# Second near inverse in two pieces, row sums on GpSimd, third o block loaded whole: the recurrence of a two-block network

## The reference, cut to what matters

```python
def step(state, xs):           # over the tokens
    sa = einsum('bhvk,bhk->bhv', state, a_t)
    state = (state * w_t[:, :, None, :] + sa[..., None] * b_t[:, :, None, :]
             + v_t[..., None] * k_t[:, :, None, :])
    return state, einsum('bhvk,bhk->bhv', state, r_t)
...
y = groupnorm_per_head(y) * ln_w + ln_b
y = y + sum(r * k * r_k, per head) * v          # bonus
return (y * g) @ w_o, v_first
```

## Time and profile before

| | |
|---|---|
| median of 3 runs | 1130.73 us |
| profiled execution, its own time | 1129.51 us |
| span of the profiled execution | 1127.5 us |
| TensorE, VectorE, ScalarE, GpSimd busy | 97%, 72%, 49%, 4% of the span |
| mean granted clock of TensorE | 0.995 of full speed |

### The profile page before, as it was taken

How to read it: one execution, slowest core, us unless ns; L and a number is a source line. 1 busy time by engine, 2 the same in 40 slices (tenths; PEclk the granted TensorE clock), 3 DMA queues, 4 the chain that set the end, 5 groups by cost and what they waited for, 6 DMA issues and landing times.

```text
span 1127.5 us, 18637 instructions
## 1 busy us (share of the span) xinstructions
PE 1096.3 (97%) x7454; PEld 914.5 (81%) x7454; DVE 816.5 (72%) x1161; ACT 553.5 (49%) x690; POOL 43.3 (4%) x50
## 2 busy tenths in 40 slices
PE   9999999999999887899999999999999999999998
PEld 7887888889778667787888888798977888989896
DVE  4664544538579795979999987999997977555554
ACT  6545633436455425364334356465554756444443
POOL 0000000000000420101111100000000000000000
PEclk9999999999999989999999999999999999999999
DMA  9585456453344221649989963374540654564633
GB/s 337 192 267 187 152 183 223 157 179 112 113 149 136 74 42 41 260 153 374 341 321 343 347 212 115 111 226 149 167 149 2 202 161 133 177 207 166 208 127 112
DMA packets 138141, 205.86 MB, mean 183 GB/s; under 512 B 19592, under 2 KB 95645, under 8 KB 138078
## 3 DMA queue, kind: packets, MB, share of 16 engines
q1 hardware_dynamic: 130644, 177.63, 47.9%
q0 software_dynamic: 6560, 25.19, 5.9%
q10 hardware_dynamic: 874, 2.15, 0.5%
HBM read 202.33 MB, written 1.57 MB: 181 GB/s over the span
## 4 chain that ended last, share of the span: by engine, by line
PE 86%; DVE 8%; ACT 2%; DMA 2%; issue 1%; ACTq 0%; DVEq 0%
PE ps L749 24%; PE ps L751 24%; PE ps L750 24%; PE ps L975 2%; DVE wl L2532 1%; PE ps L1193 1%; PE ps L1632 1%; DMA raw<-in_ab_w_in 1%; PE ps L826 1%; PE ps L1108 1%; PE ps L1460 1%; PE ps L1107 1%; PE ps L1132 1%; PE ps L1614 1%; DVE wide L2646 1%
## 5 line engine op out<-in xcount | busy, mean ns | idle before, releaser
L2532 DVE TENSOR_TENSOR wl<-raw,wh 128x2048 fp32r<-128x2048 f32 (+2 forms) x154 | 345.4, 2248 | 98.5 <-ACT wh L1755 98.1
L749 PE MATMUL ps<-wh,xh 128*128 128x512 f32 (+3 forms) x856 | 339.0, 396 | 2.7 <-DVE wl L2532 1.4
L751 PE MATMUL ps<-wl,xh 128*128 128x512 f32 (+3 forms) x856 | 332.2, 388 | 0.0
L750 PE MATMUL ps<-wh,xl 128*128 128x512 f32 (+3 forms) x856 | 332.0, 388 | 0.0
L1755 ACT ACTIVATE wh<-raw 128x2048 fp32r<-128x2048 f32 (+2 forms) x154 | 286.7, 1878 | 41.0 <-PE ps L751 31.0
L749 PEld LDWEIGHTS ps<-wh,xh 128*128 128x128 f32 x856 | 161.4, 189 | 39.3 <-issue 2.4
L751 PEld LDWEIGHTS ps<-wl,xh 128*128 128x128 f32 x856 | 161.3, 188 | 34.8
L750 PEld LDWEIGHTS ps<-wh,xl 128*128 128x128 f32 x856 | 161.5, 189 | 33.3 <-issue 1.0
L749 PE MATMUL ps<-wh,gh 128*128 128x512 f32 x288 | 114.1, 396 | 0.8 <-DVE wl L2532 0.8
L751 PE MATMUL ps<-wl,gh 128*128 128x512 f32 x288 | 113.8, 395 | 0.0
L750 PE MATMUL ps<-wh,gl 128*128 128x512 f32 x288 | 113.6, 395 | 0.0
(11 more groups left out here) (448 smaller groups left out, 1307.1 us busy)
## 6 DMA issues: line engine op xcount, KB each, us to landing
wide<-in_w_ada POOLq DMA_DIRECT2D x24, 1024.0 KB, 9.2
raw<-in_ffn_w_gate SPq DMA_DIRECT2D x44, 512.0 KB, 4.4
raw<-in_ffn_w_up SPq DMA_DIRECT2D x44, 512.0 KB, 5.5
raw<-in_ffn_w_down SPq DMA_DIRECT2D x22, 1024.0 KB, 5.0
raw<-in_w_mlp_in SPq DMA_DIRECT2D x16, 1024.0 KB, 7.3
raw<-in_w_mlp_out SPq DMA_DIRECT2D x16, 1024.0 KB, 5.1
raw<-in_w_in SPq DMA_DIRECT2D x16, 512.0 KB, 4.8
raw<-in_w_in SPq DMA_DIRECT2D x8, 1024.0 KB, 5.0
```

What stands on the lines that cost most here:

```text
L749: pe.matmul(o, lh, rh, start=start, stop=False)
L750: pe.matmul(o, ll, rh, start=False, stop=False)
L751: return pe.matmul(o, lh, rl, start=False, stop=stop)
L2532: v.tensor_tensor(wl[:, s, 0:width], raw[:, s, 0:width], f32(wh[:, s, 0:width]), ALU.subtract).then_inc(lo_ready[s], 1)
```

## The change

1. `near_blocks` keeps only its two multiplications. The sums are made by GpSimd in `near_rows(g)`: an addition of 256 elements in each partition, then one of 128. `near_in` waits for these. GpSimd runs `near_rows(0)`, `(1)` after the first four fold steps, and `(2)`, `(3)` after the other four.
2. VectorE takes `mask_b` of a group right behind its `near_blocks`.
3. GpSimd's gate steps no longer wait for `near(0)`; those of the second half wait for both `y1_out(0)` and `(1)`.
4. `near` stops after the left product for corners of 8. The right product (`near_last`) follows at once for the first inverse, and for the second only after `r4_out(1)`. The halves of the first and the second o block are split later on VectorE.
5. SyncE issues `a_columns((2, 3))` ahead of `near_out(1)`, and the third o block as one load of 1 MB; ScalarE splits it between `gkv_out(2)` and `gkv_out(3)` instead of after `r1_out(3)`.
6. The four near buffers are allocated last in SBUF, so what lay behind them moves down by 3456 bytes in each partition.

```diff
@@ make_plan
-    for (n, k), s, dmas in zip(O_ORDER, (2, 0, 1, 2), (1, 1, 4, 1)):
+    for (n, k), s, dmas in zip(O_ORDER, (2, 0, 1, 2), (1, 1, 1, 1)):
@@ SyncE, recurrence_loads
                 near_in(1)
+                a_columns((2, 3))
                 near_out(1)
-                a_columns((2, 3))
                 sp.wait_ge(S("gate_T"), B("gate_T") + 4)
-                in_pieces(("o",) + O_ORDER[2], 2)
+                in_place(("o",) + O_ORDER[2])
@@ SyncE, near_in
-                sp.wait_ge(S("wkv.nc"), B("wkv.nc") + 2 * hh + 2)
+                sp.wait_ge(S("near_rows"), B("near_rows") + 4 * hh + 4)
@@ GpSimd
+            def near_rows(g):
+                blocks = tmps[g]["xt"].rearrange("p (y u b c) -> p y u b c", y=2, u=4, b=4)
+                pairs = tmps[g]["xt"].rearrange("p (u n) -> p u n", u=8)
+                rows = NEAR_ROWS(W, g // 2).rearrange("p (y g u c) -> p y g u c", y=2, g=2, u=4)[:, :, g % 2]
+                pool.wait_ge(S("wkv.nc"), B("wkv.nc") + g + 1)
+                nc.gpsimd.tensor_tensor(pairs[:, :, 0:32], pairs[:, :, 0:32], pairs[:, :, 32:64], ALU.add).then_inc(S("near_rows"), 1)
+                pool.wait_ge(S("near_rows"), B("near_rows") + 2 * g + 1)
+                nc.gpsimd.tensor_tensor(rows, blocks[:, :, :, 0, :], blocks[:, :, :, 1, :], ALU.add).then_inc(S("near_rows"), 1)
...
+                if hh == 0:
+                    near_rows(0)
+                    near_rows(1)
+            near_rows(2)
+            near_rows(3)
...
-            pool.wait_ge(S("wkv.near"), B("wkv.near") + 1)
             for hh in range(2):
...
                 pool.wait_ge(S("gate_out"), B("gate_out") + 2 * (hh + 1))
+                if hh:
+                    pool.wait_ge(S("wkv.y1"), B("wkv.y1") + 2)
@@ ScalarE
             for g in (0, 2):
                 if g == 2:
                     gkv_out(2)
+                    act.wait_ge(S("fold"), B("fold") + 16)
+                    split_in_place(("o",) + O_ORDER[2])
                     gkv_out(3)
...
                 r1_out(g + 1)
-                if g == 2:
-                    act.wait_ge(S("fold"), B("fold") + 16)
-                    split_in_place(("o",) + O_ORDER[2])
@@ VectorE, near_blocks
-                link(m)
-                rows = NEAR_ROWS(W, g // 2).rearrange("p (y g u c) -> p y g u c", y=2, g=2, u=4)
-                for y in range(2):
-                    m = v.tensor_reduce(rows[:, y, g % 2], ..., AX_X, ALU.add)
@@ VectorE, near
+                left_product(4)
+                right_product(4)
+                left_product(8)
+
+            def near_last():
+                right_product(8, last=True)
@@ VectorE, inverse_out
+                else:
+                    v.wait_ge(S("near_rows"), B("near_rows") + 2 * g + 6)
@@ VectorE, the order
             for g in (0, 2):
-                for step in (near_blocks, mask_b, mask_k, mask_x):
+                for i in (g, g + 1):
+                    near_blocks(i)
+                    mask_b(i)
+                for step in (mask_k, mask_x):
                     step(g)
                     step(g + 1)
                 if g == 0:
                     near(0)
+                    near_last()
...
                 y1_out(g)
-                if g == 0:
-                    split_in_place(first, 0)
-                else:
+                if g == 2:
                     centre(0, 0)
                 y1_out(g + 1)
...
                 r4_out(g)
-                if g == 0:
-                    split_in_place(first, 1)
-                    split_in_place(second, 0)
-                else:
+                if g == 2:
                     centre(0, 1)
                     variance(0, 0)
                     variance(0, 1)
                 r4_out(g + 1)
                 if g == 0:
-                    split_in_place(second, 1)
+                    near_last()
+                    split_in_place(first, 0)
                 else:
                     gated(0, 0)
                 q_out(g)
-                if g == 2:
+                if g == 0:
+                    split_in_place(first, 1)
+                else:
                     gated(0, 1)
                 q_out(g + 1)
...
                 state_out(g)
                 state_out(g + 1)
+                if g == 0:
+                    split_in_place(second, 0)
+                    split_in_place(second, 1)
```

More of the change, by code:

```diff
@@ L123 @@
     "pool_1": (("ones", 1), ("fold", 16)),
-    "pool_2": (("lowr_one", 1), ("near_zero", 1), ("near_unit", 1)),
+    "pool_2": (("lowr_one", 1), ("near_zero", 1), ("near_unit", 1), ("near_rows", 8)),
     "pe_1": (("cols_T", 1), ("y_T", 4)),
@@ L359, in build @@
         posi = sb("posi", [P, NT], I32)
+        near_m = sb("near_m", [P, NEAR])
+        near_u = sb("near_u", [P, NEAR])
+        near_c = sb("near_c", [P, 2 * P])
+        near_p = sb("near_p", [P, 64])
         ps = ctx.enter_context(nc.psum_tensor("ps", [P, 8, 512], F32))
@@ L504, in in_place @@
                   .then_inc(raw_loaded[s], 16)
-            def in_pieces(name, g, pieces=range(4)):
-                s, use, _, _ = plan.at[name]
-                sp.wait_ge(w_used[s], use)
-                for a in pieces:
-                    step = ("wkv.gkv", "wkv.mt", "wkv.r1", "wkv.m2")[a]
-                    sp.wait_ge(S(step), B(step) + g + 1)
-                    r0, n0 = name[2] * 512 + a * P, name[1] * 512
-                    sp.dma_start(wl_plain[:, s * SLOT + a * 512:s * SLOT + (a + 1) * 512], SRC["o"][r0:r0 + P, n0:n0 + 512])\
-                      .then_inc(raw_loaded[s], 16)
             def recurrence_loads():
@@ L2990, in mask_k, with corners, near_part, small_products @@
                                 mask_two("strict_st", "upto_st"), ALU.mult).then_inc(S("wkv.gk"), 1)
+            def corners(s):
+                k = 8 // s
+                u, m = [t[:, :].rearrange("p (k z) -> p k z", k=k)[:, :, 0:32 * s].rearrange("p k (i c) -> p k i c", c=16) for t in (near_u, near_m)]
+                return u[:, :, 0:s, 0:s], u[:, :, 0:s, s:2 * s], u[:, :, s:2 * s, s:2 * s], m[:, :, 0:s, s:2 * s]
+            def near_part(s):
+                return near_p[:, 0:8 * s].rearrange("p (k i c) -> p k i c", i=s, c=s)
+            def small_products(s, a, b, o):
+                k = 8 // s
+                products = W(8, 0, k * s ** 3).rearrange("p (k i c j) -> p k i c j", k=k, i=s, c=s)
+                for n in range(k):
+                    m = v.tensor_tensor(products[:, n], a[:, n].unsqueeze(2).to_broadcast([P, s, s, s]),
+                                        b[:, n].rearrange("p j c -> p c j").unsqueeze(1).to_broadcast([P, s, s, s]), ALU.mult)
+                link(m)
+                for n in range(k):
+                    m = v.tensor_reduce(o[:, n], products[:, n], AX_X, ALU.add)
+                return m
+            def left_product(s):
+                _, _, u22, m12 = corners(s)
+                link(small_products(s, m12, u22, near_part(s)))
+            def right_product(s, last=False):
+                u11, u12, _, _ = corners(s)
+                m = small_products(s, u11, near_part(s), u12)
+                if last:
+                    m.then_inc(S("wkv.near"), 1)
+                else:
+                    link(m)
             def near(hh):
@@ L2998, in near @@
                     v.wait_ge(S("near_unit"), B("near_unit") + 1)
-                def corners(s):
-                    k = 8 // s
-                    u, m = [t[:, :].rearrange("p (k z) -> p k z", k=k)[:, :, 0:32 * s].rearrange("p k (i c) -> p k i c", c=16) for t in (near_u, near_m)]
-                    return u[:, :, 0:s, 0:s], u[:, :, 0:s, s:2 * s], u[:, :, s:2 * s, s:2 * s], m[:, :, 0:s, s:2 * s]
                 _, u12, _, m12 = corners(1)
```

22 lines of the change are left out of this document (2 added, 20 removed).

## The result

The changed kernel takes 1110.3 us (median of 4 runs, 1109.84 to 1110.7) against 1130.54 us (4 runs, 1129.19 to 1132.53): ratio 0.982, 95% interval 0.980 to 0.983. The profiled execution took 1110.59 us, with a span of 1108.4 us.

The account below looks back on a forecast made before the run. TensorE, busy 97% of the span, was taken to bound the kernel, with gains only at its holes in the recurrence: 6.3 + 4.8 = 11.1 us, 1130.7 - 11.1 = 1119.6 us, range 1117.0 to 1125.0.

Parts of the forecast that it names:

- (d): GpSimd row sums at r us each lose 4(r - 1.05) - 1 us, deciding from 4.1; chance 0.06 including other losses.
- Part 1: Row sums to GpSimd: `gram_v(1)` 2.2 us earlier, second pair 2.2 us earlier, `inverse_out(0)` able to start 3.9 us earlier.
- rival (b): VectorE and GpSimd collide further, with GpSimd sums of 2.5 us: gain only 5.7 us, 1125.0 us; chance 0.08.
- Part 2: GpSimd gate steps no longer behind `near(0)`: they collide with `inverse_out`, yet `off_1(0)` comes 6.4 us earlier, its hole 0.8.
- Part 3: Second inverse's last product moved: `out_parts(0)` 8.4 us earlier, but VectorE waits at `inverse_out(2)`, so `gram_v(2)` only 6.8 us earlier.
- rival (a): The wait moves on: third block lands last, or the clock falls ahead of `gram_v(2)`; gain 8.4 us, 1122.3; chance 0.16.
- Part 4: Splits last, third block whole: `next_state(0,2)` 6.3 us earlier, and the hole ahead of `off_2(2)` gone for 4.8 us more.
- Rival (c): Loads pace the stage at 520 to 540 us, so the gain is given back: 1130.7 us; chance 0.03.

Follow-up runs that it names:

- place_only: The kernel before, with only the four near buffers allocated last in SBUF: 1120.73 us against 1130.49, ratio 0.991.
- order_only: The changed kernel with the four near buffers back between `h` and `xh`: 1121.0 us, ratio 0.992.
- sums_dve: The changed kernel with the row sums back on VectorE and GpSimd's gate steps waiting for `near_blocks(3)`: 1114.76 us, ratio 0.986.
- near_whole: The changed kernel with `near_last` directly behind `near(1)` again, the second inverse in one piece: 1109.64 us, ratio 0.982.
- third_old: The changed kernel with the third o block again in four pieces, split by ScalarE after `r1_out(3)`: 1113.55 us, ratio 0.985.
- third_early: The changed kernel with `state_out` ahead of `inverse_out(2)`, and the third o block loaded ahead of `near_out(1)` and split earlier: 1108.63 us, ratio 0.981.

## Why the prediction was off, point by point

**The step that failed** is the sentence "New buffers' places in SBUF cost nothing by any row." It excluded a loss for want of a row, and never asked for a gain. `place_only` puts the placement at 9.8 us, more than the 9.3 us by which the forecast of 1119.6 missed 1110.3. Without it the rest of the forecast would have looked right: `order_only` took 1121.0 us, inside the forecast's own 1118.0 to 1121.7. No row of before could give the size: the kernel has these operands in one place only. But it could have been bounded: a nanosecond on 3240 products is up to 3.2 us, so the price of a moved operand of `mm3` should have had a range, not a zero.

The forecast's own range has a slip of arithmetic as well: for sums of 1.5 us it takes off 1.3 us "by the formula of (d)", which gives 4 x 0.45 - 1 = 0.8. This changed nothing, as one `near_rows` took 1.28 us.

**Part 1 was right.** `gram_v(1)` came at 376.49 + 4.2 = 380.7 (forecast 380.6), `near(0)` at 384.2 (383.9), the second pair at 390.8 (390.7). One `near_rows` takes 1.28 us from the start of the first addition at 387.41 to the end of the second, not 1.05; rival (b)'s 2.5 and rival (d)'s 4.1 us are far away. `sums_dve` agrees with the part: 4.5 us, where the prediction has VectorE 3.9 us ahead after both pairs.

**Part 2 was right.** `inverse_out(0)` started at 397.4 (397.3) and collided: its two multiplications took 2.75 us, while GpSimd worked from 390.47 without a gap until 395.6; the next two took 0.75. At half speed that pair would have taken 1.5 us, twice its 0.75; one engine waiting for the other's whole instructions, which the prediction took, fits the 2.75. The Trainium skill ("SBUF — State Buffer", section "Who interferes with whom") has the same rule, and the trace agrees: 2.75 us against 0.75 for the same pair of instructions. `off_1(0)` came at 406.2 (405.8), its hole was 0.35 us (0.8 forecast) and it took 1.10 us, full clock.

**Part 3 had the right order of waits and was 1.3 us short.** `out_parts(0)` came at 410.7 (410.05) and the product held back ended at 413.5 (413.3). The way over DRAM was forecast as 5.3 us (its three terms, 1.7, 1.7 and 2.3, add up to 5.7) and took 6.2: from its end at 409.3 to `inverse_out(2)` at 415.51. The two transfers of L544 took 2.05 us to issue, not the 1.27 of the earlier trace rows. So `gram_v(2)` came at 422.3 and not at 421.05, after a hole of 2.40 us and not 1.6, and the clock fell to 0.50, where the prediction wanted it at 1.00 nearly throughout. That is the second case of rival (a), held at 0.16, in the place that it named; the recurrence's 9.0 us lie nearer to its 8.4 than to 11.1. The front half gave 4.5 us (9.77 at `gram_v(2)` and 8.71 at the product at 434.26, less 4.23), not 6.3. `near_whole` adds what the prediction didn't ask: taking this move out of the changed kernel costs nothing measurable.

**Part 4 was right.** The hole ahead of `off_2(2)` is gone and the stretch from the product at 434.26 to the end of the recurrence gave 13.23 - 8.71 = 4.5 us (4.8 forecast); `third_old` says 3.3 by the medians. The split ran at 424.0 in the prediction's times, not 422.3, and ScalarE did not wait for it: it was later because `gkv_out(2)` was, behind the hole.

**Sum.** Recurrence 9.0 us of the 11.1 forecast (9.5 by the medians of `order_only`), placement 9.8 where zero was written. The two measured alone make 19.3 us, both together 20.2; the 0.9 between them is within what the runs spread.

Rival (c), time given back later, had 0.03 and did not happen to the order's gain, which stays between 9.26 and 9.44 from the end of the recurrence on in `order_only`. It did happen to the placement's (2.2 us between 532 and 550 us), and to that of `third_early`.

## What to carry to other kernels

When an edit adds, removes or moves a buffer, work out for the dense products of TensorE how far apart their two operands now start, and whether that is still a multiple of 256 bytes, the one step told apart here; put a range on it. Before believing in a gain or loss, split "where" from "when": run the new allocation with the old order. And compare the same product in both traces through the whole span: a gain that grows steadily where nothing was changed isn't scheduling.

On an engine that works in order, a wait that is removed can come back at the next slow way (here the trip over DRAM, and after that a late packet of instructions); ask which instruction behind it doesn't need that data and could go first. When the profile says "issue", look at the queue of instruction packets beside the large loads.

## What the hardware showed unexpectedly

- 512-column float32r products start every 227 ns when their two operands, the weights and the streamed columns, lie a multiple of 256 bytes apart, and every 232 ns when they lie 128 bytes off that (six placements and both orders; mean lengths 390 and 395 ns; 9.8 us of 1130 between `place_only` and the kernel before). It is the distance and not the place of the weights alone: with `spare` as the streamed operand the weights that are 128 bytes off are fast beside a `spare` that is off as well.
- TensorE stood still for 2.92 us with all its data there: a 16 KB packet of the instruction queue began 2.3 us late, as the last of a 1 MB load went through, and the product came 1.5 us after the packet's end. With the load issued 7.2 us earlier the stop was 0.30 us. That the load held the packet back is read from one trace and this one pair of kernels.
- A small GpSimd addition costs much of a large one: 0.74 us for 256 elements and 0.46 for 128, against 1.27 for 512 in the earlier trace rows.
